# A decoder step on one core: product-key expert gates by indexed 4-byte adds in DRAM instead of one-hot products

## The chip, the core and the metric

The kernel runs on one core of a Trainium2 chip. The metric is device time in microseconds for one launch of the whole program. Five engines work beside each other and meet only at semaphores: TensorE (PE in the rows, with its weight loads as PEld), VectorE (DVE), ScalarE (ACT), GpSimd (POOL) and the queue SP, which only issues DMAs. POOL can issue DMAs too, and it alone issues the indexed ones.

## The reference, cut to what matters

One decoder layer over T = 592 tokens (16 meta tokens, 512 prompt tokens, 8 sequences of 8): mixers (gated linear attention and SSD), then the expert layer "PEER", then a norm. The change touches the expert layer, which works on the 576 tokens that aren't meta tokens:

```python
s1 = einsum('thd,kd->thk', q[:, :, 0], sub_k1); s2 = einsum('thd,kd->thk', q[:, :, 1], sub_k2)   # 8 heads, 128 keys each
v1, i1 = top_k(s1, 16);  v2, i2 = top_k(s2, 16)
cand = (v1[..., :, None] + v2[..., None, :]).reshape(n_tok, 8, 256)
sc, ci = top_k(cand, 16)
e = take_along_axis(i1, ci // 16) * 128 + take_along_axis(i2, ci % 16)    # one of 16384 experts, 128 slots a token
gate = softmax(sc)
hid = einsum('tkd,td->tk', u[e], t);  out = einsum('tk,tkd->td', gate * gelu(hid), v[e])
```

## The kernel before, in words

The kernel computes the expert layer densely for most tokens: it forms the hidden value of every token with all 16384 experts, multiplies by a gate matrix that is zero except at the chosen experts, and multiplies by all of v. TP = 576 tokens take part in the u products; TA = 448 of them go through the dense v products, and the last TBK = 128 are done by gathering the 128 chosen rows of v each ("slots").

**The u stage.** 128 blocks n, each with 128 experts. SP loads the block's u into one of four places of `ring` (`load_u`). ACT copies it rounded to fp32r (the high part, `split_u`, line 1030), another engine subtracts to get the low part (POOL, line 1573), and PE runs `split_product` (line 776): 8 x 3 x 2 = 48 products of 288 columns. `usp` has two places for the pair. ACT applies gelu into `gl` and SP stores it to `hidden_scratch` in DRAM.

**Routing.** Beside the first blocks, in five tiles of up to 128 tokens, PE computes `scores(i)` (16 small products), ACT copies them to `s12`, and DVE finds the top 16 of each half and head, the top 16 of 256 candidates, and by comparisons and sums (lines 1419 to 1423) the expert numbers e1, e2; then it divides the gates by their sum. ACT does the exponential (line 1072) in between. `scores(i)` stands ahead of quad 3i of the u blocks (a quad is four blocks). Tile 0 is the 128 tokens of the gathered path. The picks of tiles 1 to 4 are turned by PE (`turn_picks`) into e1T, e2T, gT.

**Gates by one-hot products.** From quad 17 on, two blocks of 16 tokens a quad, 28 in all: DVE makes a one-hot of e1 and one of e2 (lines 1450, 1451, each 128 x 2048), multiplies the first by two of three bf16 parts of the gate (line 1454), POOL by the third (line 1577), PE runs `gate_block` (line 835, 48 bf16 products), ACT copies the result to `stage` (line 1081), and SP stores it to `gates_scratch` (1 MB each), laid out (16 groups, 128, 448 tokens, 8).

**The v stage.** 128 blocks: SP loads v, the hidden block (`xn`) and, once for eight blocks, gates (`G`, 1.8 MB); DVE multiplies hidden by gate (`gate`, line 1472), ACT and DVE split v and the product in high and low parts, PE runs `second(n)` (line 866): 24 products of 448 columns. POOL issues the 128 + 128 gathers for the last 128 tokens (`pick_hid` line 1600, `pick_row` line 1593), and DVE adds the rows (line 1496). After the last block follow the add to h, a norm and the store.

**Ahead of all that**, SP loads the weights of 36 projections one by one into `ring` (`load_w`, line 394, 512 KB each, four places), each once PE is done with the projection four before it. Every instruction of an engine's list runs in the order written; the lists are unrolled or run in `Fori` loops.

## Time and profile before

| | us |
|---|---|
| median of 3 runs | 2213.4 |
| lowest, highest of 3 | 2199.16, 4156.74 |
| the profiled execution's own time | 2213.47 |
| span of the profiled execution | 2211.7 |

The profile is of one execution; its span starts and ends with the core's instructions, and 1.8 us of its own time lie around it. A row of a group of instructions gives its busy time, the mean of one in ns, and then the idle time of the engine just before them and what ended it. A row of a timeline gives start, duration (both us), what ran, and in brackets how long its engine had been idle and for whom. In the table by stretches, the bracketed x is the count of instructions, PEclk the clock that TensorE was granted as a share of full speed, and the last two the mean busy share of the 16 DMA engines and their rate.

### The profile page before, as it was taken

To read this page: it belongs to the slowest core of one execution; us is meant where nothing else is said; L and a number is where in the kernel's file an instruction comes from. 1 tells how busy PE (TensorE), PEld (TensorE's weight loads), DVE (VectorE), ACT (ScalarE), POOL (GpSimd) and SP (SyncE) were. 2 spreads that over 40 slices of the span, in tenths; PEclk is the share of its full clock that TensorE was granted. 3 is DMA by queue.
4 is the path that set the end of the run, shared out by engine and by line. 5 is a ranking of instruction groups with operands and counts; after the bars stand their busy time and mean duration, and the time that the engine had idled before them with its cause. 6 is when DMAs were issued, how large, how long until landed. Compare 5 with 4: busy or idle time off the path is not lost.

```text
span 2211.7 us, 34613 instructions
## 1 busy us (share of the span) xinstructions
PE 2108.4 (95%) x13720; PEld 1925.0 (87%) x13720; DVE 1576.2 (71%) x2188; ACT 659.0 (30%) x1062; POOL 1007.1 (46%) x452
## 2 busy tenths in 40 slices
PE   6999998798999999999999999999999999999996
PEld 3578777666999999999999998999899999999995
DVE  2335364635098898894899999992588888888884
ACT  2224112211223323323333332323333333333331
POOL 0023210201333333343887887973866665666300
PEclk8999997799999999999999999999999999999998
DMA  3011012022233333333455455546898989989861
GB/s 139 10 58 67 29 31 79 1 82 82 87 119 120 119 134 120 119 129 121 160 166 164 161 164 161 166 155 214 305 319 310 338 306 330 319 299 347 311 212 44
DMA packets 169054, 364.94 MB, mean 165 GB/s; under 512 B 18529, under 2 KB 92786, under 8 KB 166258
## 3 DMA queue, kind: packets, MB, share of 16 engines
q1 hardware_dynamic: 146418, 296.26, 38.9%
q0 software_dynamic: 22528, 67.19, 8.7%
q8 instruction: 74, 1.21, 0.2%
q14 instruction: 34, 0.28, 0.0%
HBM read 290.21 MB, written 73.18 MB: 164 GB/s over the span
## 4 chain that ended last, share of the span: by engine, by line
PE 55%; issue 24%; POOL 13%; DVE 5%; ACT 1%; DMA 1%; SPq 0%; POOLq 0%; DVEq 0%; ACTq 0%
PE bank L866 28%; POOL usp L1573 10%; PE bank L517 8%; PE bank L776 5%; PE bank L746 3%; POOL oneA L1577 3%; PE bank L551 2%; PE bank L503 1%; DVE oneA L1454 1%; PE bank L622 1%; PE bank L835 1%; DVE sq L1131 1%; PE bank L593 1%; DVE xn L1134 1%; PE bank L638 1%
## 5 line engine op out<-in xcount | busy, mean ns | idle before, releaser
L776 PE MATMUL bank<-xh,usp 128*128 128x288 f32 x4320 | 761.5, 297 | 7.0 <-POOL usp L1573 3.7
L776 PEld LDWEIGHTS bank<-xh,usp 128*128 128x128 f32 x4320 | 638.7, 189 | 9.5 <-POOL usp L1573 4.9
L866 PE MATMUL bank<-W,vsp 128*128 128x448 f32 x3072 | 635.0, 368 | 1.1 <-DVE W L1482 1.1
L866 PEld LDWEIGHTS bank<-W,vsp 128*128 128x128 f32 x3072 | 576.5, 188 | 59.3 <-issue 1.4
L1573 POOL TENSOR_TENSOR usp<-ring,usp 128x1024 fp32r<-128x1024 f32 x128 | 405.6, 3173 | 391.3 <-ACT usp L1030 391.3
L776 PE MATMUL bank<-xl,usp 128*128 128x288 f32 x2160 | 462.7, 296 | 0.0
L776 PEld LDWEIGHTS bank<-xl,usp 128*128 128x128 f32 x2160 | 348.6, 189 | 0.0
L1030 ACT ACTIVATE usp<-ring 128x1024 fp32r<-128x1024 f32 x128 | 135.6, 1060 | 611.9 <-PE bank L776 611.9
L1593 POOL DMA_INDIRECT picked<-in_v,row_index x128 | 173.9, 1359 | 181.4 <-DVE acc L1496 163.9
L1477 DVE TENSOR_TENSOR vsp<-ring,vsp 128x1024 fp32r<-128x1024 f32 x128 | 157.7, 1232 | 129.1 <-ACT vsp L1094 115.2
L1454 DVE TENSOR_TENSOR oneA<-hotA,gparts 128x2048 bf16<-128x2048 bf16 x56 | 226.7, 4087 | 0.0
L517 PE MATMUL bank<-xn,ring 128*128 128x296 f32 (+1 forms) x672 | 215.8, 445 | 10.8 <-DVE xn L1134 7.8
L1600 POOL DMA_INDIRECT hid_b<-hidden_scratch,hid_index x128 | 180.6, 1411 | 49.5 <-issue 38.7
L1094 ACT ACTIVATE vsp<-ring 128x1024 fp32r<-128x1024 f32 x128 | 135.5, 1058 | 130.6 <-PE bank L866 116.2
L1098 ACT ACTIVATE W<-sq 128x448 fp32r<-128x448 f32 x128 | 74.3, 581 | 296.9 <-DVE sq L1472 294.7
L1472 DVE TENSOR_TENSOR sq<-xn,G 128x448 f32<-128x448 f32 x128 | 140.5, 1098 | 31.0 <-DMA xn<-hidden_scratch 31.0
L1496 DVE SCALAR_TENSOR_TENSOR acc<-picked,w_b,acc 128x1024 f32<-128x1024 f32 x126 | 161.6, 1288 | 0.2
L1577 POOL TENSOR_TENSOR oneA<-hotA,gparts 128x2048 bf16<-128x2048 bf16 x28 | 152.1, 5433 | 0.0
L517 PEld LDWEIGHTS bank<-xn,ring 128*128 128x128 f32 x672 | 115.3, 194 | 39.7 <-issue 17.8
L1450 DVE TENSOR_TENSOR hotA<-cst,e1T 128x2048 bf16<-128x2048 f32 x28 | 111.3, 3976 | 15.2 <-PE bank L835 15.2
L1451 DVE TENSOR_TENSOR oneB<-cst,e2T 128x2048 bf16<-128x2048 f32 x28 | 114.7, 4096 | 0.0
L1533 POOL TENSOR_TENSOR E<-E,qT 128x2048 f32<-128x2048 f32 (+1 forms) x7 | 29.1, 4163 | 181.0 <-ACT qT L908 114.2
(237 smaller groups left out, 2001.8 us busy)
## 6 DMA issues: line engine op xcount, KB each, us to landing
ring<-in_u SPq DMA_DIRECT2D x128, 512.0 KB
ring<-in_v SPq DMA_DIRECT2D x128, 512.0 KB
hidden_scratch<-gl SPq DMA_DIRECT2D x128, 288.0 KB, 2.1
gates_scratch<-stage SPq DMA_DIRECT2D x28, 1024.0 KB, 5.6
G<-gates_scratch SPq DMA_DIRECT2D x16, 1792.0 KB
xn<-hidden_scratch SPq DMA_DIRECT2D x128, 224.0 KB
ring<-in_wproj SPq DMA_DIRECT2D x36, 512.0 KB
h<-in_xT SPq DMA_DIRECT2D x16, 296.0 KB, 4.5
```

The costliest lines, as they stand in the source:

```text
L517: mm = pe.matmul(bank[2 * (n % 2) + x][:, 0:half], ring[:, n % 4, k * P:(k + 1) * P], src[:, k, at + x * half:at + (x + 1) * half], start= ...
L776: mm = pe.matmul(bank[b + y][:, 0:PHALF], w, src[:, k, y * PHALF:(y + 1) * PHALF], start=(k == 0 and w is hi and src is xh), stop=(k == KT ...
L866: mm = pe.matmul(bank[(k + 4) % 8][:, 0:TA], w, W[:, n % 4, z, :], start=(n == 0 and w is hi and z == 0), stop=(n == NE - 1 and w is lo))
L1030: act.activation(usp[:, j % 2, 0, :], ring[:, j % 4, :], ACT.Copy).then_inc(uhi_ready, 1)
L1454: ins = dve.tensor_tensor(oneA[:, x, z, :, :], hotA[:, x, :, :], bc(gparts[:, z, bass.ds(b * TB, TB)], 2, NK), ALU.mult)
L1472: dve.tensor_tensor(sq[:, n % 2, 0:TA], xn[:, n % 8, 0:TA], G[n // GRP % 2][:, :, n % GRP], ALU.mult).then_inc(gated, 1)
L1477: dve.tensor_tensor(vsp[:, n % 4, 1, :], ring[:, n % 4, :], vsp[:, n % 4, 0, :].bitcast(F32), ALU.subtract).then_inc(vlo_ready, 1)
L1496: ins = dve.scalar_tensor_tensor(acc[:, x % 2, :], picked[:, x % NROW, :], w_b[:, x:x + 1], acc[:, x % 2, :], ALU.mult, ALU.add)
L1573: pool.tensor_tensor(usp[:, j % 2, 1, :], ring[:, j, :], usp[:, j % 2, 0, :].bitcast(F32), ALU.subtract).then_inc(ulo_ready, 1)
L1577: pool.tensor_tensor(oneA[:, j, 2, :, :], hotA[:, j, :, :], bc(gparts[:, 2, bass.ds((b + j) * TB, TB)], 2, NK), ALU.mult).then_inc(third_r ...
L1593: pool.indirect_dma_start(picked[:, x % NROW, :], None, rows_of_v, bass.IndirectOffsetOnAxis(ap=row_index[:, x:x + 1], axis=0)).then_inc(r ...
L1600: pool.indirect_dma_start(hid_b[:, x:x + 1], None, hid_flat, bass.IndirectOffsetOnAxis(ap=hid_index[:, x:x + 1], axis=0)).then_inc(picked_ ...
```

## The change

- The four temporaries of the one-hot way, `turn_picks`, `gate_block`, `gates_out`, `store_gates`, `one_hots` and POOL's third product go. `gates_scratch` becomes (128 blocks, 128, 448).
- A tile `zero` is set once by POOL. SP writes zeros over `gates_scratch` with 32 DMAs, four behind each of the weight loads 4 to 11, in pieces of 224 floats.
- Tiles are renumbered: the four of the dense path come first (128, 128, 128, 64 tokens), the gathered 128 tokens last. `scores(0)` stands ahead of the first quad, `scores(i + 1)` behind quad 4i; ACT copies tile i + 1's scores after quad 4i + 1 and the exponential of tile i.
- DVE keeps each tile's gates (`gate_val`) and their places (`gate_at`). POOL adds them with indexed DMAs of one column each, a 4-byte float for each token: 128 of them a tile (8 heads x 16), 512 in all. Between two heads of one tile it waits until the first head's 16 have landed; the later four heads of tile i - 1 and the first four of tile i are issued alternately.
- POOL makes the low parts of u for blocks 0 to 15; DVE makes the other 112, in the midst of the routing of tiles 1 to 4, one for each 6.0 us of work by the program's own count (`after`), the rest in a row after it. `usp` has four places instead of two, and ACT's high part is for block n + 4 instead of n + 2, and follows the gelu.
- `G` is loaded block by block (224 KB each) into eight places: the first eight by POOL once all adds have landed, the others by SP ahead of `load_hid`.

```diff
@@ SP
+            for n in range(4):
                 load_w(n)
+            sp.wait_ge(zero_ready, 1)
+            for n in range(4, 12):
+                load_w(n)
+                for g in (2 * n - 8, 2 * n - 7):
+                    for y in range(2):
+                        sp.dma_start(gates_dram[g * GRP:(g + 1) * GRP, :, y * (TA // 2):(y + 1) * (TA // 2)].rearrange("n p t -> p n t"),
+                                     zero[:, :, :].broadcast_to([P, GRP, TA // 2])).then_inc(zeroed, 16)
...
+            def load_gates(n):
+                sp.dma_start(G[:, n % 8, :], gates_dram[n, :, :]).then_inc(hid_loaded[n % 8], 16)
...
-            load_gates(1)
+            wait_gates_added(sp)
@@ PE
+            scores(0)
+            for i in range(TILES):
+                pooled = ROUTE_QUADS * i < POOL_SPLITS // 4
+                quad(ROUTE_QUADS * i, pooled, first=(i == 0))
+                if i + 1 < TILES:
+                    scores(i + 1)
                 with pe.Fori(ROUTE_QUADS * i + 1, ROUTE_QUADS * (i + 1)) as q:
-                    quad(q)
+                    quad(q, pooled)
+            with pe.Fori(ROUTE_QUADS * TILES, NE // 4) as q:
+                quad(q, False)
@@ ACT
-                    split_u(n + 2, j + 2, q)
                     gelu(n, j, None if first else q)
+                    split_u(n + 4, j, q + 1)
...
                 quad(ROUTE_QUADS * i, first=(i == 0))
+                quad(ROUTE_QUADS * i + 1)
                 act.wait_ge(sm_arg, i + 1)
                 act.activation(e12[0:r, 2, :, :], e12[0:r, 2, :, :], ACT.Exp).then_inc(sm_exp, 1)
+                if i + 1 < TILES:
+                    copy_scores(i + 1)
@@ DVE
+            def split_u(n):
+                dve.wait_ge(uhi_ready, n + 1)
+                dve.tensor_tensor(usp[:, n % NU, 1, :], ring[:, n % 4, :], usp[:, n % NU, 0, :].bitcast(F32), ALU.subtract
+                                  ).then_inc(ulo_ready, 1)
+            def after(us):
+                worked[0] += us
+                while worked[0] >= PITCH:
+                    split_u(next_split[0])
+                    next_split[0] += 1
+                    worked[0] += 1.3 - PITCH
...      # after(1.5) behind each of the 16 top16 of 128, after(3.3) behind each of the 8 of 256,
...      # after(3.3) and after(7.5) twice in the picks; tiles 1 to 4 only
+                    dve.tensor_tensor(gate_val[0:r, i, :, :], e12[0:r, 2, :, :], bc(den[0:r, 1, :], 2, TOPK), ALU.mult
+                                      ).then_inc(gates_ready, 1)
+                    link(dve.scalar_tensor_tensor(w_b[0:r, :], e2, float(NK), e1, ALU.mult, ALU.add))
+                    dve.tensor_scalar(gate_at[0:r, i, :], w_b[0:r, :], float(TA), col, ALU.mult, ALU.add
+                                      ).then_inc(gates_ready, 1)
+            for n in range(next_split[0], NE):
+                split_u(n)
...
-                dve.tensor_tensor(sq[:, n % 2, 0:TA], xn[:, n % 8, 0:TA], G[n // GRP % 2][:, :, n % GRP], ALU.mult
+                dve.tensor_tensor(sq[:, n % 2, 0:TA], xn[:, n % 8, 0:TA], G[:, n % 8, :], ALU.mult
@@ POOL
+            for n in range(POOL_SPLITS):
+                pool.wait_ge(uhi_ready, n + 1)
+                pool.tensor_tensor(usp[:, n % NU, 1, :], ring[:, n % 4, :], usp[:, n % NU, 0, :].bitcast(F32), ALU.subtract
+                                   ).then_inc(ulo_first, 1)
+            def add_gates(i, hh):
+                r = peer_rows(i)
+                if hh > 0:
+                    pool.wait_ge(gates_added[i], 16 * TOPK * hh)
+                for x in range(hh * TOPK, (hh + 1) * TOPK):
+                    pool.indirect_dma_start(gates_flat, bass.IndirectOffsetOnAxis(ap=gate_at[0:r, i, x:x + 1], axis=0),
+                                            gate_val[0:r, i, hh, x - hh * TOPK:x - hh * TOPK + 1], None, compute_op=ALU.add
+                                            ).then_inc(gates_added[i], 16)
+            pool.wait_ge(zeroed, 16 * 2 * NGRP)
+            for i in range(TILES):
+                if i < TILES - 1:
+                    pool.wait_ge(gates_ready, 2 * (i + 1))
+                for hh in range(PH // 2):
+                    if i >= 1:
+                        add_gates(i - 1, PH // 2 + hh)
+                    if i < TILES - 1:
+                        add_gates(i, hh)
+            wait_gates_added(pool)
+            for n in range(8):
+                pool.dma_start(G[:, n, :], gates_dram[n, :, :]).then_inc(g_first[n // 4], 16)
```

## Rows read from the trace of the kernel before

**Rows 1.** The page, part 1: busy time of each engine, share, instructions

```profile
PE 2108.4 (95%) x13720; PEld 1925.0 (87%) x13720; DVE 1576.2 (71%) x2188; ACT 659.0 (30%) x1062; POOL 1007.1 (46%) x452
```

**Rows 2.** Busy time by stretch: stretch, length, PE, PEld, DVE, ACT, POOL, PEclk, DMA, GB/s

```profile
600.80:1060.00 459.20, 457.44 (x3448) 455.82 (x3449) 386.01 (x1156) 142.69 (x254) 175.33 (x70) 1.00 0.36 123
1060.00:1510.00 450.00, 434.42 (x3967) 430.35 (x3966) 422.34 (x104) 146.15 (x276) 370.66 (x83) 0.98 0.51 164
...
1544.60:2180.50 635.90, 634.82 (x3074) 576.60 (x3073) 501.47 (x515) 205.60 (x253) 354.49 (x256) 1.00 0.83 296
2180.50:2211.70 31.20, 12.92 (x42) 8.37 (x40) 15.60 (x20) 7.66 (x11) 0.00 (x0) 0.75 0.20 79
```

**Rows 3.** ACT's timeline: high parts of u, each started by a finished block

```profile
617.29 1.06 ACT L1030 ACTIVATE usp<-ring 128x1024 fp32r<-128x1024 f32 x1 [3.31 <-PE bank L776]
...
674.98 1.07 ACT L1030 ACTIVATE usp<-ring 128x1024 fp32r<-128x1024 f32 x1 [4.82 <-PE bank L776]
...
681.29 1.06 ACT L1030 ACTIVATE usp<-ring 128x1024 fp32r<-128x1024 f32 x1 [4.66 <-PE bank L776]
...
691.29 1.06 ACT L1030 ACTIVATE usp<-ring 128x1024 fp32r<-128x1024 f32 x1 [4.51 <-PE bank L776]
```

**Rows 4.** Groups of instructions between 1060 and 1510 us

```profile
L1454 DVE TENSOR_TENSOR oneA<-hotA,gparts 128x2048 bf16<-128x2048 bf16 x52 | 213.3, 4141 | 0.0
...
L835 PE MATMUL bank<-oneB,oneA 128*128 128x128 bf16 x1344 | 86.1, 228 | 13.1 <-DVE oneA L1454 13.1
L835 PEld LDWEIGHTS bank<-oneB,oneA 128*128 128x128 bf16 x1344 | 81.2, 103 | 16.1 <-issue 14.5
```

**Rows 5.** DVE's timeline in the routing of tile 0, beside POOL's low parts

```profile
606.41 0.29 DVE L1390 MAX8 v<-s 128x8 f32<-128x128 f32 x1 [51.54 <-ACT s L1064]
...
631.53 2.38 DVE L1404 TENSOR_TENSOR cand<-v 128x256 f32<-128x256 f32 x1
...
636.20 0.41 DVE L1404 TENSOR_TENSOR cand<-v 128x256 f32<-128x256 f32 x1
...
659.42 0.29 DVE L1411 TENSOR_TENSOR e<-v 128x128 f32<-128x128 f32 x1
...
684.67 0.28 DVE L1425 TENSOR_REDUCE den<-e 128x8 f32<-128x128 f32 x1 [3.17 <-ACT e L1072]
```

**Rows 6.** The page, part 5: the low part of v on DVE

```profile
L1477 DVE TENSOR_TENSOR vsp<-ring,vsp 128x1024 fp32r<-128x1024 f32 x128 | 157.7, 1232 | 129.1 <-ACT vsp L1094 115.2
```

**Rows 7.** POOL's timeline: a low part of u beside routing

```profile
612.03 2.40 POOL L1573 TENSOR_TENSOR usp<-ring,usp 128x1024 fp32r<-128x1024 f32 x1 [5.57 <-ACT usp L1030]
```

**Rows 8.** POOL's timeline, indexed gathers of 128 x 4 bytes; last row, DVE's timeline

```profile
1550.66 0.95 POOL L1600 DMA_INDIRECT hid_b<-hidden_scratch,hid_index  x1 [0.30 <-issue]
...
1556.93 0.95 POOL L1600 DMA_INDIRECT hid_b<-hidden_scratch,hid_index  x1 [0.30 <-issue]
1558.19 1.67 POOL L1600 DMA_INDIRECT hid_b<-hidden_scratch,hid_index  x1 [0.30 <-issue]
...
1575.45 1.22 POOL L1593 DMA_INDIRECT picked<-in_v,row_index  x1 [0.30 <-issue]
...
1557.81 1.23 DVE L1477 TENSOR_TENSOR vsp<-ring,vsp 128x1024 fp32r<-128x1024 f32 x1 [7.92 <-issue]
```

**Rows 9.** Groups on POOL between 1600 and 2050 us

```profile
L1600 POOL DMA_INDIRECT hid_b<-hidden_scratch,hid_index x104 | 150.1, 1443 | 31.7 <-issue 31.7
L1593 POOL DMA_INDIRECT picked<-in_v,row_index x103 | 139.0, 1350 | 130.6 <-DVE acc L1496 116.4 <-issue 12.5 <-DVE acc L1493 1.7
```

**Rows 10.** The page, part 6, DMA issues: count, KB each, us from issue to landing

```profile
hidden_scratch<-gl SPq DMA_DIRECT2D x128, 288.0 KB, 2.1
gates_scratch<-stage SPq DMA_DIRECT2D x28, 1024.0 KB, 5.6
```

**Rows 11.** SP's timeline, weight loads 4 to 11, and ACT's copy of projection 11

```profile
105.86 65.26 SPq L394 DMA_DIRECT2D ring<-in_wproj  x8
...
222.06 0.72 ACT L908 ACTIVATE sz<-bank 128x296 f32<-128x296 f32 x2
```

More of the change, by code:

```diff
@@ L125, in constants @@
         "eps": np.full((P, 1), EPS),
-        "gcol": TA + r[:, None],
+        "column": np.stack([peer_cols(i).start + r for i in range(TILES)], axis=1),
     }
@@ L157, in build @@
         cst = sb(base, "cst", [P, CONST_N])
+        zero = sb(base, "zero", [P, 1, TA // 2])
         prm = sb(base, "prm", [P, PARAM_N])
@@ L289, in build @@
         hid_stored = [sem(f"hid_stored{s}") for s in range(4)]
-        g_loaded = [sem(f"g_loaded{s}") for s in range(2)]
+        g_first = [sem(f"g_first{s}") for s in range(2)]
         stored = sem("stored")
@@ L822, in quad @@
                     mm.then_inc(hid_done, 1)
-                    if b is not None and j < 2:
-                        gate_block(b + j, j, first=(isinstance(b, int) and b + j == 0))
-            def gate_block(b, x, first=False):
-                pe.wait_ge(one_hot_ready, b + 1)
-                pe.wait_ge(third_ready, b + 1)
-                for q in range(TB // 4):
-                    if not first:
-                        pe.wait_ge(gate_copied, b * (TB // 4) + q - 3)
-                    for t in range(4):
-                        for z in range(3):
-                            mm = pe.matmul(bank[4 + q][:, t * NK:(t + 1) * NK], oneA[:, x, z, 4 * q + t, :],
-                                           oneB[:, x, 4 * q + t, :], start=(z == 0), stop=(z == 2))
-                    mm.then_inc(gate_done, 1)
@@ L1044, in quad, with copy_scores @@
                     act.wait_ge(hid_done, n + 1)
-                    split_u(n + 2, j + 2, q)
                     gelu(n, j, None if first else q)
-                    if b is not None and j < 2:
-                        gates_out(b + j, j, first=isinstance(b, int))
-            def copy_picks(i):
-                act.wait_ge(e_turned, i)
-                for x, dst in enumerate((e1T, e2T, gT)):
-                    ins = act.activation(dst[:, peer_cols(i)], bank[4][:, x * P:x * P + peer_rows(i)], ACT.Copy)
-                ins.then_inc(e_copied, 1)
-            split_u(0, 0, 0)
-            split_u(1, 1, 0)
-            for i in range(TILES):
+                    split_u(n + 4, j, q + 1)
+            for j in range(4):
+                split_u(j, j, 0)
+            def copy_scores(i):
                 r = peer_rows(i)
@@ L1526, in _ @@
         def _(pool):
+            pool.memset(zero[:, :, :], 0.0).then_inc(zero_ready, 1)
             pool.wait_ge(proj_act, 2)
@@ L1567, in _ @@
                                    ).then_inc(qlo_ready, 1)
-            def quad(q, b=None):
-                for j in range(4):
-                    pool.wait_ge(uhi_ready, q * 4 + (j + 1))
-                    pool.tensor_tensor(usp[:, j % 2, 1, :], ring[:, j, :], usp[:, j % 2, 0, :].bitcast(F32), ALU.subtract
-                                       ).then_inc(ulo_ready, 1)
-                    if b is not None and j < 2:
-                        pool.wait_ge(one_hot_step, b + (j + 1))
-                        pool.tensor_tensor(oneA[:, j, 2, :, :], hotA[:, j, :, :],
-                                           bc(gparts[:, 2, bass.ds((b + j) * TB, TB)], 2, NK), ALU.mult
-                                           ).then_inc(third_ready, 1)
```

214 lines of the change are left out of this document (68 added, 146 removed).

## The prediction, made before the changed kernel ran

> **What bounds the kernel now.** I read the page's busy times first, then the table by stretches, then the waits and timelines of each stretch. TensorE is busy 95% of the span [rows 1], but the stages differ. In the u stage with routing (600.8 to 1060) and in the v stage (from 1544.6, 635.9 us) PE hardly pauses; the v stage is bound by PE's own products, DVE at 79% and the DMA engines at 83% beside it [rows 2]. The middle, 1060 to 1510, is where one-hot gates are made: DVE is busy 422 of 450 us, POOL 371, and PE is 16 us short of full [rows 2]. So PE sets the time nearly everywhere, and what can be gained is PE work that goes away plus those waits.
>
> The price of a block of u comes from ACT's timeline. A high part starts when a block is done, and nine blocks lie between 617.29 and 674.98: 57.7 / 9 = 6.41 us a block. The step from 681.29 to 691.29 has `scores` in it: 10.0 - 6.4 = 3.6 us [rows 3].
>
> **PE after the change.** The stage runs from 600.8 to 1544.6, 943.8 us [rows 2]. Without gate products and turns there remain 128 blocks x 6.41 = 820.5 and five `scores` x 3.6 = 18.0, together 838.5 us. That is 105.3 us less, if nothing new holds PE. Cross-check: 28 gate blocks with 86.1 us of busy product records (they overlap a little, so some 75 to 86) and the waits in front of them, 13.1 for DVE and up to 16.1 for loads of weights [rows 4]: 104 to 115. The v stage would then begin at 600.8 + 838.5 = 1439.3 instead of 1544.6.
>
> **DVE as maker of low parts.** One low part is 1024 columns, two inputs, fp32r out: the same shape as the low part of v, 1.23 us [rows 6]. Routing of tile 0 takes 606.4 to 659.4 up to the exponential's argument and ends at 681.5 in its picks (684.67 less the 3.17 of waiting) [rows 5]: 75.1 us, with POOL's low parts in its way (the same `cand` operation takes 2.38 or 0.41 us [rows 5]). The program counts 16 x 1.5 + 8 x 3.3 + 2 x (3.3 + 7.5) = 72.0 us for it, and takes a low part for each 4.7 of them (6.0 - 1.3): 15.3 a tile. In real time that is at most 4.7 x 75.1 / 72.0 + 1.3 = 6.2 us a low part, under PE's 6.41. So DVE keeps up, and mostly waits for ACT's high part, which comes three blocks ahead of need (19 us of cover). The 2 us of small operations at a tile's end fit in there. Cost 0; if the pitch were 7 us instead, 61 low parts would bring (7 - 6.41) x 61 - 19 = 17 us. ACT waits for a tile's exponential argument with the gelus of later blocks behind it. DVE reaches it with low part 26 (tile 1), and ACT stands at it after block 23; PE stalls only from block 26, for whose banks it needs gelu 24. A few us of slack at worst, cost 0. SP's load of u for block n + 4 waits for DVE instead of POOL, and still has more than one block of time, against 2 to 6 us that loads and stores take to land [rows 10]. One low part in the first sixteen costs POOL 2.40 us of each 6.41 [rows 7], nothing for PE.
>
> **Zeroing.** 32 stores, 29.4 MB, go in between loads 4 to 11 on one queue. Loads 4 to 11 start within 65.3 us from 105.9, and projection 11, the last behind zeros, must be fed some 11 us before ACT copies it at 222.1 [rows 11]. 29.4 + 4.2 MB in about 105 us is 320 GB/s. The v stage moves 296 GB/s at a share of 0.83, so 357 GB/s at full share [rows 2]; the 1 MB gate stores in 512-byte pieces take 5.6 us, 187 GB/s with the latency in it, 300 without 2.1 us of it [rows 10]. At 357 there is no stall; at 300, 33.6 / 0.3 = 112 us, 7 us late; at 187 it would be 75 us late, which would leave 2183. The pieces here are 896 bytes and many DMAs are in flight, which is nearer to the first: I take 0, and keep 75 as the far end.
>
> **POOL's adds** decide. An indexed add does not occur in the trace; the nearest is the indexed gather of 128 x 4 bytes. Alone, with DVE idle, five periods take 1556.93 - 1550.66: 1.25 us each (0.95 busy, 0.30 between). When DVE starts its two-input operations at 1557.8, nine take 17.26: 1.92 each [rows 8]. Over the v stage the mean is (1.443 + 1.350) / 2 + 0.31 = 1.70, with DVE busy 79% [rows 2, 9]. So DVE's two-input operations stretch them, by (1.70 - 1.25) / 0.79 = 0.57 us per unit of such share. In the u stage DVE has such work for about 37 of 98 us a tile (15.3 low parts x 1.23 = 19, candidates 8 x 0.41 = 3, and an estimated 15 of the 22 us of picks), then 1.23 of each 6.41: 1.25 + 0.57 x 0.38 = 1.46 us an add while routing lasts, 1.25 + 0.57 x 0.19 = 1.36 after. I take these. Bounds: 1.25 and 1.70.
>
> The Trainium skill says of this ("SBUF — State Buffer", section "SBUF: two separate sides") that GpSimd, which writes the descriptors, is fully blocked from a shared port while such a DVE operation runs. Here the trace agrees only in part: at a DVE share of three quarters the period grows 1.5 times, where full blocking would make it four times. By that rule the adds would take about 1.25 / 0.62 = 2.0 us during routing and 1.25 / 0.81 = 1.54 after it, and the time would be about 2260, the upper end of the first rival.
>
> Now the chain. Block 1 ended at 617.3 [rows 3]; POOL's last low part (15) follows block 11, at 617.3 + 10 x 6.41 + 3.6 = 685.0, plus some 4 us for gelu, high part (1.06) and low part (2.40): 689. Gates of tile 0 are ready at 684, the picks' end and 2 us of small operations. Four heads of tile 0: 64 x 1.46 = 93, and three waits for landing; a store's 2.1 us [rows 10] each: 788. Tile 1's gates are ready at 684 + 15.3 x 6.41 + 3.6 = 786, tile 2's at 888, so from here POOL is never starved. 128 more: 187, to 975. The next 128: 79 until routing ends at 1091, 49 x 1.36 = 67 after, to 1158. The next 128: 174, to 1332. The last 64 x 1.36 = 87 and four landings, 8: 1427. First loads of G: four issues and a landing, 4 x 1.25 + 2.1 = 7, then `gate` and the split of W, 3 us: W is ready at 1437. PE is free at 1439.3. The adds just fit. In general W is ready at 715.5 + 512 a, a being the mean period of an add (here 1.41); each 0.1 us of a is 51 us. Tile 3 has 64 tokens, which may make 128 of the adds cheaper; no row shows it, bounds 0 to 60 us earlier.
>
> **The v stage** keeps its 24 products a block. `G` now moves in 1792-byte pieces like `xn`, same bytes, 0 us; DVE's `gate` can only get cheaper. The tail from 2180.5 [rows 2] stays.
>
> **Sum.** 2211.7 - 105.3 = 2106.4 of span; the profiled execution took 1.8 us more than its span, so 2108.2, and I say 2108. That execution (2213.47) is the median of the runs shown (2213.4), whose lowest is 14 us under it.
>
> **Rivals.**
> - *Adds late but bearable*: a from 1.44 to 1.70, as in the v stage. Time 2108 + 512 x (a - 1.41): at 1.70, 715.5 + 870.4 = 1585.9, which is 41 us later than the v stage began before, 2255. For it: all gathers beside a busy DVE cost this. Against it: DVE has half that load here. It costs more than it brings from a = 1.62 on.
> - *An add is dearer than a gather* (ends slower). An add must fetch what lies in DRAM beside what it brings, so POOL has more to write for it. If it writes twice as much: 2 x 0.95 + 0.30 = 2.20 alone, about 2.36 with DVE: 715.5 + 1208 = 1924, 379 us later than before, 2593. It decides from a = 1.71 (2% slower). The mirror of it is a landing that outlasts 16 adds of the other tile (23 us); then the waits between heads pace it. For it: nothing in the trace shows an add. Against: the DMA engines are idle two thirds of this time [rows 2]. The Trainium skill ("Collectives: The Full Stack", section "The bandwidth ceiling: the fold count and why AG ≠ RS ≠ AR") says that an add emits two read descriptors per piece where a copy emits one, and that this halved the rate; no row here shows it, and by it the time would be this rival's.
> - *PE isn't freed*: low parts on DVE at 7 us or the zero stores late, 10 to 30 us given back: 2118 to 2138. Speaks against it: 6.2 us by the sum above.
>
> **Chances.** Forecast (adds hidden or nearly, 2095 to 2125) 0.48; given back in part, 2125 to 2169, 0.12; within 2% of before, 2169 to 2258, 0.15 (the upper part of the first rival); slower, 0.25. Two per cent, 44 us, is about what a measurement of this kernel can tell from no change. Faster 0.60, same 0.15, slower 0.25. The likeliest case's own range is 2090 to 2125. The range for 8 in 10 runs from 2090, by the spread of the runs and cheaper half tiles, to 2260, the gather's worst price; dearer adds stay outside.
>
> **What would show it.** Right: PE's blocks of 6.41 us throughout, v products starting near 1440, POOL's adds at 1.3 to 1.5 us in a row until about 1425, no stall of PE around 110 to 220. Wrong: PE idle ahead of the v stage for the G loads, with POOL still adding, and a period over 1.5 us; idle gaps in the add stream at head ends (landing); PE waiting for low parts from DVE; PE waiting for `ring` near 150 to 220.

## The result, and the profile after

| | us |
|---|---|
| changed kernel, median of 4 runs (lowest, highest) | 2424.61 (2419.52, 2429.45) |
| kernel before, median of 4 runs on the same chip | 2207.03 |
| ratio, with its 95% interval | 1.100 [1.096, 1.105] |
| forecast | 2108 |

One of the four executions of the kernel before took 4156.74 us; it stands apart from the other three (2199.16 to 2213.4) and is left out of the ratio. The change makes the kernel 10% slower; the time lies 317 us above the forecast. The page of the changed kernel (busy times, then groups with busy us, mean ns, idle time before and its releaser, then a DMA row with KB and us to landing):

```profile
PE 2027.9 (84%) x12364; PEld 1845.5 (76%) x12364; DVE 1158.1 (48%) x2191; ACT 607.7 (25%) x943; POOL 1335.7 (55%) x833
...
L1521 POOL DMA_INDIRECT gates_scratch<-gate_val,gate_at x512 | 851.3, 1663 | 184.5 <-issue 155.9
L823 PE MATMUL bank<-W,vsp 128*128 128x448 f32 x3072 | 643.4, 370 | 315.3 <-DVE W L1420 299.2
...
L1410 DVE TENSOR_TENSOR sq<-xn,G 128x448 f32<-128x448 f32 x128 | 79.2, 619 | 317.7 <-DMA G<-gates_scratch 317.7
...
gates_scratch<-zero SPq DMA_DIRECT2D x32, 896.0 KB, 10.5
```

PE's busy share falls from 95% [rows 1] to 84%, although its busy time fell by 80 us. It waits once for 299.2 us, for W; W's maker waits for `G`, and `G` for the last of 512 adds. The adds hold POOL for 851 us, 1.66 us each. The table by stretches (columns as in [rows 2]) sets the same in time:

```profile
0.00:600.80 600.80, 535.71 (x2952) 421.15 (x2953) 242.84 (x387) 146.20 (x252) 97.36 (x41) 0.92 0.32 108
600.80:1439.00 838.20, 836.61 (x6302) 835.03 (x6301) 451.28 (x1263) 246.76 (x426) 658.99 (x370) 1.00 0.58 128
1439.00:1736.60 297.60, 0.00 (x0) 0.00 (x0) 4.06 (x6) 1.18 (x3) 236.18 (x167) 0.50 0.19 6
1736.60:2395.80 659.20, 643.04 (x3071) 581.12 (x3072) 444.29 (x516) 205.91 (x253) 343.15 (x256) 0.98 0.84 285
```

The u stage is full and ends at 1437 (last product 1436.98). Then of all engines only POOL has work for 298 us. The v stage takes 659.2 us instead of 635.9 [rows 2]. So there are two losses: 297.4 us by which the v stage begins later than 1439.3, and 23.3 us inside it. With a tail 0.4 us shorter, 2108.2 + 297.4 + 23.3 - 0.4 = 2428.5, and that execution took 2426.6 of span and 1.8 around it, 2428.4. The two losses are the whole difference between forecast and time.

**The first loss.** POOL's timeline of the changed kernel (start, us, and the idle time before), beside DVE's low parts and, in the last two rows, with no DVE work:

```profile
1271.28 1.55 POOL L1521 DMA_INDIRECT gates_scratch<-gate_val,gate_at  x1 [0.31 <-issue]
1273.14 2.31 POOL L1521 DMA_INDIRECT gates_scratch<-gate_val,gate_at  x1 [0.30 <-issue]
1275.75 1.55 POOL L1521 DMA_INDIRECT gates_scratch<-gate_val,gate_at  x1 [0.30 <-issue]
1277.60 1.55 POOL L1521 DMA_INDIRECT gates_scratch<-gate_val,gate_at  x1 [0.30 <-issue]
1279.45 2.39 POOL L1521 DMA_INDIRECT gates_scratch<-gate_val,gate_at  x1 [0.30 <-issue]
...
1499.10 1.55 POOL L1521 DMA_INDIRECT gates_scratch<-gate_val,gate_at  x1 [0.30 <-issue]
1500.96 1.55 POOL L1521 DMA_INDIRECT gates_scratch<-gate_val,gate_at  x1 [0.30 <-issue]
```

and DVE's timeline of the same stretch:

```profile
1272.80 1.23 DVE L1338 TENSOR_TENSOR usp<-ring,usp 128x1024 fp32r<-128x1024 f32 x1 [5.09 <-ACT usp L987]
1279.19 1.23 DVE L1338 TENSOR_TENSOR usp<-ring,usp 128x1024 fp32r<-128x1024 f32 x1 [5.17 <-ACT usp L987]
```

An add of 128 tokens holds POOL for 1.55 us where the gather of the same size held it for 0.95 [rows 8]; the pause of 0.30 is the same. That is a period of 1.85, and 1.73 for the tile of 64 tokens (1.43 busy). A low part that is running when an add starts lengthens the add, by 0.76 and 0.84 us in these rows and by 1.02 at most after routing; the mean distance between 1100 and 1400 us is 2.12. The rows also show by what rule. The low part of 1279.19 ends at 1280.42 and the add beside it at 1281.84, 1.42 us later; the one of 1272.80 ends at 1274.03 and its add at 1275.45, again 1.42 later. After 1095 us an add starts beside a running low part 47 times, and 46 times it ends 1.41 to 1.44 us behind the low part's end. So the add stands still until the low part is over and has only 0.13 of its 1.55 us behind it by then. An add that has started first is not lengthened, and neither is the low part (POOL's timeline, then DVE's):

```profile
1118.96 1.55 POOL L1521 DMA_INDIRECT gates_scratch<-gate_val,gate_at  x1 [0.30 <-issue]
```

```profile
1119.20 1.23 DVE L1338 TENSOR_TENSOR usp<-ring,usp 128x1024 fp32r<-128x1024 f32 x1 [3.81 <-ACT usp L987]
```

**The second loss.** PE's timeline at the start of the v stage of the changed kernel:

```profile
1736.65 25.25 PE L823 MATMUL bank<-W,vsp 128*128 128x448 f32 x111 [299.24 <-DVE W L1420]
...
1772.10 0.53 PE L823 MATMUL bank<-W,vsp 128*128 128x448 f32 x1 [0.68 <-issue]
1774.20 0.53 PE L823 MATMUL bank<-W,vsp 128*128 128x448 f32 x1 [1.57 <-issue]
...
1784.00 0.53 PE L823 MATMUL bank<-W,vsp 128*128 128x448 f32 x1 [0.85 <-issue]
1786.10 74.18 PE L823 MATMUL bank<-W,vsp 128*128 128x448 f32 x351 [1.57 <-issue]
```

From 1762 to 1786 PE starts 17 products, mostly one each 1.4 to 2.8 us, where it did 111 in the 25 us before, and the profile shows nothing that it waits for ("issue"). POOL's timeline of the same kernel shows what runs meanwhile:

```profile
1760.60 0.95 POOL L1551 DMA_INDIRECT hid_b<-hidden_scratch,hid_index  x1 [0.30 <-issue]
1761.85 0.94 POOL L1544 DMA_INDIRECT picked<-in_v,row_index  x1 [0.31 <-issue]
1763.10 0.95 POOL L1551 DMA_INDIRECT hid_b<-hidden_scratch,hid_index  x1 [0.30 <-issue]
...
1780.60 0.95 POOL L1551 DMA_INDIRECT hid_b<-hidden_scratch,hid_index  x1 [0.31 <-issue]
1815.52 0.95 POOL L1544 DMA_INDIRECT picked<-in_v,row_index  x1 [33.98 <-DVE acc L1431]
```

Indexed gathers go 1.25 us apart, without a break, until 1781; PE recovers at 1786. The experiments take up both losses.

### The profile page after: what moved, and what is told of

It is laid out like the page before. It is cut to its first block, busy times and chain, and to the rows that moved or that the text cites. A ratio compares the mean times of both kernels' runs of the same rounds, so it can differ in the third digit from the quotient of the medians.

```text
span 2426.6 us, 31564 instructions
## 1 busy us (share of the span) xinstructions
PE 2027.9 (84%) x12364; PEld 1845.5 (76%) x12364; DVE 1158.1 (48%) x2191; ACT 607.7 (25%) x943; POOL 1335.7 (55%) x833
## 3 DMA queue, kind: packets, MB, share of 16 engines
q0 software_dynamic: 88576, 69.29, 17.7%
## 4 chain that ended last, share of the span: by engine, by line
PE 51%; POOL 35%; issue 8%; DVE 3%; DMA 2%; ACT 1%; SPq 0%; DVEq 0%; POOLq 0%; ACTq 0%
POOL gates_scratch L1521 34%; PE bank L823 27%; PE bank L510 8%; PE bank L769 5%; PE bank L739 3%; DMA gates_scratch<-gate_val,gate_at 2%; PE bank L544 2%; PE bank L496 1%; PE bank L615 1%; DVE sq L1071 1%; PE bank L586 1%; DVE xn L1074 1%; PE bank L631 1%; PE bank L726 1%; PE bank L696 0%
## 5 line engine op out<-in xcount | busy, mean ns | idle before, releaser
L1521 POOL DMA_INDIRECT gates_scratch<-gate_val,gate_at x512 | 851.3, 1663 | 184.5 <-issue 155.9
L823 PE MATMUL bank<-W,vsp 128*128 128x448 f32 x3072 | 643.4, 370 | 315.3 <-DVE W L1420 299.2
L769 PE MATMUL bank<-xh,usp 128*128 128x288 f32 x4320 | 752.0, 296 | 1.4 <-DVE xl L1326 1.4
L1338 DVE TENSOR_TENSOR usp<-ring,usp 128x1024 fp32r<-128x1024 f32 x112 | 136.8, 1221 | 341.9 <-ACT usp L987 318.2
L1544 POOL DMA_INDIRECT picked<-in_v,row_index x128 | 149.8, 1171 | 216.4 <-DVE acc L1434 165.5
L1410 DVE TENSOR_TENSOR sq<-xn,G 128x448 f32<-128x448 f32 x128 | 79.2, 619 | 317.7 <-DMA G<-gates_scratch 317.7
L994 ACT ACTIVATE gl<-bank 128x288 f32<-128x288 f32 x256 | 91.3, 409 | 542.9 <-PE bank L769 484.8
L1551 POOL DMA_INDIRECT hid_b<-hidden_scratch,hid_index x128 | 193.3, 1510 | 48.0 <-issue 38.7
L1420 DVE TENSOR_TENSOR W<-sq,W 128x448 fp32r<-128x448 f32 x128 | 79.0, 617 | 0.1
L1502 POOL TENSOR_TENSOR xl<-xn,xh 128x576 fp32r<-128x576 f32 x4 | 7.7, 1951 | 119.9 <-ACT xh L973 119.9
```

Of the source, the lines that this page charges most:

```text
L769: mm = pe.matmul(bank[b + y][:, 0:PHALF], w, src[:, k, y * PHALF:(y + 1) * PHALF], start=(k == 0 and w is hi and src is xh), stop=(k == KT ...
L823: mm = pe.matmul(bank[(k + 4) % 8][:, 0:TA], w, W[:, n % 4, z, :], start=(n == 0 and w is hi and z == 0), stop=(n == NE - 1 and w is lo))
L994: ins = act.activation(gl[:, j, y * PHALF:(y + 1) * PHALF], bank[2 * (j % 2) + y][:, 0:PHALF], ACT.Gelu_apprx_tanh)
L1338: dve.tensor_tensor(usp[:, n % NU, 1, :], ring[:, n % 4, :], usp[:, n % NU, 0, :].bitcast(F32), ALU.subtract).then_inc(ulo_ready, 1)
L1521: pool.indirect_dma_start(gates_flat, bass.IndirectOffsetOnAxis(ap=gate_at[0:r, i, x:x + 1], axis=0), gate_val[0:r, i, hh, x - hh * TOPK:x ...
L1544: pool.indirect_dma_start(picked[:, x % NROW, :], None, rows_of_v, bass.IndirectOffsetOnAxis(ap=row_index[:, x:x + 1], axis=0)).then_inc(r ...
```

## The experiments

All kernels are the changed kernel with one edit; e12 joins the edits of e3 and e9. The kernel before took 2195.1 us beside the first eight, 2201.2 beside e9 to e11.

**e1: plain indexed writes in place of adds (gates that meet on one place aren't summed); e2: gathers of the same places (no gate is written at all).**

```diff
 pool.indirect_dma_start(gates_flat, IndirectOffsetOnAxis(ap=gate_at[0:r, i, x:x + 1], axis=0),
-                        gate_val[...], None, compute_op=ALU.add)
+                        gate_val[...], None)                                          # e1
-pool.indirect_dma_start(gates_flat, IndirectOffsetOnAxis(...), gate_val[...], None, compute_op=ALU.add)
+pool.indirect_dma_start(gate_in[0:r, i, x:x + 1], None, gates_flat, IndirectOffsetOnAxis(...))  # e2
```

> The changed kernel with its 512 indexed DMAs as plain writes instead of adds; it leaves out the sum where two heads of a token chose the same expert. In the changed kernel one add, alone on POOL, takes 1.55 us and 0.30 between (period 1.85), and 2.12 beside DVE's low parts, and PE waits 299 us. Theory A: the price lies in the adding (two things to fetch for each write). Then a plain write costs what a gather does: 0.95 us alone, period 1.25, some 1.45 beside DVE, the adds end near 1440 and the time is 2120 to 2160. Theory B: the price lies in the direction, an index on the DRAM side of a write. Then 1.55 stays, and the time stays at 2410 to 2430.

> The changed kernel with each of the 512 adds replaced by a gather of the same 128 places into SBUF, so the gates stay zero. Both theories on adding and direction: 0.95 us alone, period 1.25, 1.36 to 1.46 beside DVE as the prediction took, end near 1427, time 2105 to 2140. Rival: the u stage itself (its DMA traffic, DVE's low parts) makes indexed DMAs dear; then the gather too would take 1.5 us or more and the time would stay above 2250.

Measured: 2774.0 and 2744.1 us. The trace by line of e1 and of e2 (minimum, median, maximum in ns, first and last start):

```profile
L1521 POOL DMA_INDIRECT gates_scratch<-gate_val,gate_at x512: 891/958/1913, 688.9 to 1626.0; - x171
```

```profile
L1522 POOL DMA_INDIRECT gate_in<-gates_scratch,gate_at x512: 894/947/1931, 683.3 to 1627.8; - x171
```

Two things follow. A plain write costs what a gather does, 0.96 and 0.95 us, so the direction is free and **the accumulation is the price**: 1.55 against 0.96. The pages (part 3, packets of POOL's own queue, MB, share) show that an add is cut up finer, in the changed kernel and then in e1:

```profile
q0 software_dynamic: 88576, 69.29, 17.7%
```

```profile
q0 software_dynamic: 39424, 69.29, 7.6%
```

That is 96 packets more for each of the 512 transfers. Whether their making is what holds POOL 0.6 us longer, no run tests.

The second thing: the kernel became slower, not faster, and the last write started at 1626, although 512 x 1.26 is only 645 us. The stretch from 857 to 1020, in e1 and then in the changed kernel, both in the columns of [rows 2]:

```profile
857.00:1020.00 163.00, 37.13 (x137) 28.18 (x135) 17.10 (x83) 4.60 (x7) 122.85 (x127) 0.53 0.05 11
```

```profile
857.00:1020.00 163.00, 163.00 (x1230) 162.71 (x1229) 128.57 (x404) 54.07 (x91) 137.96 (x79) 1.00 0.59 126
```

While plain writes run 1.26 us apart, PE does 137 products instead of 1230, DVE 83 operations instead of 404, and the DMA engines move a tenth. "Starve" below stands for this. POOL starves with them: it waits 282 us in three places for `gate_at`, which the hindered routing delivers late. PE's timeline of e1 in that stretch looks like the v stage's stall above:

```profile
896.46 0.40 PE L769 MATMUL bank<-xl,usp 128*128 128x288 f32 x1 [2.40 <-issue]
899.26 0.40 PE L769 MATMUL bank<-xh,usp 128*128 128x288 f32 x1 [2.40 <-issue]
902.06 0.40 PE L769 MATMUL bank<-xh,usp 128*128 128x288 f32 x1 [2.40 <-issue]
```

That was not expected by any theory, and e5 to e7 and e9 to e11 are about it.

**e3, e4: four and six of the eight heads are added** (the gates of the others are left out).

```diff
-                eng.wait_ge(gates_added[i], 16 * PH * TOPK)
+                eng.wait_ge(gates_added[i], 16 * 4 * TOPK)
-                for hh in range(PH // 2):
+                for hh in range(4 // 2):              # 6 in e4, here and in the other lines
-                        add_gates(i - 1, PH // 2 + hh)
+                        add_gates(i - 1, 4 // 2 + hh)
```

> The changed kernel with the adds of heads 0 to 3 only (256 of 512); the gates of heads 4 to 7 are left out. Theory: POOL's stream of adds alone holds the v stage back, so 256 x 2.1 us from 689 on end near 1250, all hidden; PE goes from the u stage into the v stage at 1439 and the time is 2108 (2100 to 2125), the sum of the prediction without the adds. Rival: something else of the change (four places of usp, G loaded by block, the start of the v stage) costs too; then 2125 or more, with PE's idle time or a longer v stage showing it.

> The changed kernel with the adds of six heads (384 of 512); the gates of heads 6 and 7 are left out. Theory: the time follows the number of adds once they outlast PE's 1439 us, at the mean of 2.0 us. 128 adds fewer end 128 x 1.8 to 2.1 = 230 to 270 us earlier, near 1480, v stage from about 1490, time 2155 to 2200. Rival: the landings between heads pace the stream; then the time falls by less than 200 us, since as many heads' ends remain in the stretches that are not alternated.

Measured: 2122.5 and 2178.8 us. With 256 adds the last starts at 1241, and PE goes from u (1437.8) to v without a gap. With 384 it starts at 1476.1 and PE waits 57.2 us. From 384 to 512 adds the span grows by 2426.6 - 2177.0 = 249.6 us, 1.95 us an add: once POOL ends last, the number of adds times their period sets the time (the v stage took 1.8 us of the 249.6). In both, the v stage took 652.6 and 657.4 us: the second loss is there without the first.

**e8: a one-input operation on DVE beside the adds** (the true low part of u is left out).

```diff
-dve.tensor_tensor(usp[:, n % NU, 1, :], ring[:, n % 4, :], usp[:, n % NU, 0, :].bitcast(F32), ALU.subtract)
+dve.tensor_scalar(usp[:, n % NU, 1, :], ring[:, n % 4, :], 2.0 ** -14, None, ALU.mult)
```

> The changed kernel, with DVE's low part of u made by an operation of one input (ring x 2^-14) in place of the two-input subtraction; the true low part of u is left out. Theory A (two-input operations of DVE are what stretch an add from 1.85 to about 2.12 us): after routing, where the low parts are DVE's only work, the period goes to 1.85 to 1.90; over the stage 40 to 100 us fall away, and the time is 2320 to 2385. Rival (any operation of DVE on wide rows stretches them, or the adds stretch for another reason, the u loads or the stores of hidden rows): the period stays at 2.05 to 2.15 and the time at 2410 to 2430.

Measured: 2366.7 us; the last add starts at 1674.7 instead of 1723.0. POOL's and then DVE's timeline of e8:

```profile
1256.76 1.55 POOL L1520 DMA_INDIRECT gates_scratch<-gate_val,gate_at  x1 [0.30 <-issue]
1258.61 1.90 POOL L1520 DMA_INDIRECT gates_scratch<-gate_val,gate_at  x1 [0.30 <-issue]
```

```profile
1259.73 0.69 DVE L1338 TENSOR_SCALAR usp<-ring 128x1024 fp32r<-128x1024 f32 x1 [5.71 <-issue]
```

The mean distance between 1100 and 1400 us is 1.89, not 2.12, so DVE's low parts do stretch the adds, and theory A's numbers came in. But two inputs are not the condition: the one-input operation stretches them too, by 0.35 us here for its 0.69 us. An add that starts beside it ends 1.43 us behind its end, as with the subtraction; the shorter the operation, the fewer adds it meets and the sooner it lets them go. One difference stays open: after 1095 us the subtraction never lengthened an add that had started first, and this operation does when it starts 1.0 to 1.2 us into the add, as in these rows, but not at 0.2 to 0.4. (13 of the 62 us by which this execution is shorter than the profiled one of the changed kernel belong to the v stage, as much as PE's pace makes, see the last section.)

**e7: the picks held back.**

```diff
+            pool.wait_ge(block_done, 6)
             for x in range(TOPK):
                 pick_hid(x)
```

> The changed kernel, with POOL's picks of hidden values (16 indexed gathers in a row, 1.25 us apart) held back until block 6 of the v stage is done. Theory A (the gathers in a row starve PE at the start of the v stage, where VectorE and the weight loads are just behind): held back, they run where eight blocks of G, xn and v lie ready or DVE stretches them, the v stage goes from 659 us back to about 636 to 642, time 2400 to 2408 in place of 2425. Rival: the v stage is longer because the first blocks' loads or G come late; then it stays near 659 and the time near 2425; or the stall only moves with the gathers to block 6, again 2425.

Measured: 2431.0 us, v stage 663 us. The stall moved with the gathers, as the second half of the rival has it. PE's timeline of e7:

```profile
1736.95 52.33 PE L823 MATMUL bank<-W,vsp 128*128 128x448 f32 x239 [298.28 <-DVE W L1420]
1789.94 1.09 PE L823 MATMUL bank<-W,vsp 128*128 128x448 f32 x4 [0.66 <-issue]
...
1815.98 44.27 PE L823 MATMUL bank<-W,vsp 128*128 128x448 f32 x201 [0.17 <-issue]
```

The gathers start at 1770.6 instead of 1740.2, the stall at 1789 instead of 1762: some 20 us behind them in both. The first blocks' loads, which were the rival's first half, are not the cause: PE does 239 products without a pause before this stall.

**e9: the picks paced.** Behind each indexed gather, two memsets of POOL, each waiting for the one before.

```diff
+            def pause():
+                for _ in range(2):
+                    if paced_n[0]:
+                        pool.wait_ge(paced, paced_n[0])
+                    paced_n[0] += 1
+                    pool.memset(zero[:, 0, 0:224], 0.0).then_inc(paced, 1)
```

> The changed kernel with its 512 adds, and two memsets of 224 columns on POOL after each indexed gather of the v stage (hidden values and rows of v). Theory A (indexed transfers 1.25 us apart hold up the issue of the other engines, while those some 1.8 us apart don't): the stall of PE near 1762 to 1786 disappears wherever the gathers fall, the v stage goes from 659 to 636 to 642 us, and the time from 2425 to 2400 to 2408. Rival (the gathers as such cost that, in whatever distance, or something else of the v stage): 655 to 665 us and about 2425, as when they were held back.

Measured: 2405.9 us. PE's timeline of e9:

```profile
1736.74 637.57 PE L823 MATMUL bank<-W,vsp 128*128 128x448 f32 x3072 [298.81 <-DVE W L1420]
```

All 3072 products of the v stage run without a pause, in 637.6 us instead of 659.2. POOL has more to do than before (1508.6 us busy instead of 1335.7), and the kernel is 19 us faster: the gathers 1.25 us apart were the cause of the second loss. (Both executions have the same pace of PE, see the last section.)

**e5, e10, e6: plain writes at growing distance; e11: smaller ones.** As e1 (duplicates of a place aren't summed), with memsets behind each write, of 8 columns (e5), 224 (e10) and twice 224 (e6). e11 is e1 with 16 of the 128 tokens in each transfer (the other tokens' gates are left out).

```diff
+                    for _ in range(2):                  # once in e5 and e10
+                        if paced_n[0]:
+                            pool.wait_ge(paced, paced_n[0])
+                        paced_n[0] += 1
+                        pool.memset(zero[:, 0, 0:224], 0.0).then_inc(paced, 1)      # 0:8 in e5
-                r = peer_rows(i)
+                r = 16                                  # e11 alone, without memsets
```

> The plain indexed writes of e1, and after each of them a small memset of 8 columns on POOL that waits for the memset before it (the gates aren't accumulated, so those that fall on one place twice are left out). Its purpose is the distance between two indexed transfers: 1.26 us in e1, about 1.4 to 1.5 here. Theory A (what starves PE, ACT, DVE and SP is that the next indexed transfer is issued with no more than 0.3 us of pause, whatever it moves): the starving shrinks or disappears, the stretch of plain writes shows a PE share well over the 23% of e1, and the time falls from 2774 to below 2400. Theory B (the cost lies in each plain transfer as such, 128 pieces of 4 bytes without a read of what is there): the same 512 transfers cost PE what they cost in e1, about 580 us, whatever lies between: about 2700 to 2774.

> Plain indexed writes as in e1 and e6, with one memset of 224 columns after each (gates that fall on one place twice aren't summed). It puts the distance near 1.55 us, between 1.45, where the other engines starved, and 1.82, where they did not. If the starving ends below 1.55: writes done by about 1500, PE full from 700 to 1000 and 1100 to 1400, the v stage from 1500 to 1520, time 2160 to 2230. If it ends above: PE at half in these stretches, time 2550 to 2720. A gradual effect would lie between, with PE at 60 to 90%.

> As the run before, but two memsets of 224 columns in a row after each plain indexed write (duplicates of a place left out again), for a distance of some 1.8 us or more, that of the adds of the changed kernel when VectorE is idle (1.85). Theory A (distance between transfers decides): no starving at all; POOL is done about when the adds are done in the changed kernel, if the distance is 1.85 to 2.1, and the time is 2330 to 2450, with PE busy in the u stage as there. Theory B (cost per plain transfer): still about 580 us of lost PE time, 2700 or more.

> Plain indexed writes without a pause as in e1, but each moves 16 of the 128 tokens (the gates of the other tokens are left out). Theory P (the other engines are held up by the 128 small pieces of each transfer, 100 pieces a us): with an eighth of the pieces PE keeps its blocks of 6.4 us and the time is 2105 to 2130. Theory I (each indexed transfer that POOL issues holds them up, however small it is): the same starving, PE at half between 700 and 1000, time 2600 or more. The add's own price: 16 rows at 0.90 us or less (64 rows took 0.90, 128 rows 0.96) say that nearly all of it is fixed.

Measured (the distance is from start to start, without the waits of over 4 us; PE is its busy share of 700 to 1000 and 1100 to 1400, and the column beside it its products there as a share of the 4520 of the changed kernel; at a lower clock a product takes longer, so the busy share hides part of the loss):

| | distance, us: median, mean | POOL busy with one | PE busy | PE's products | time, us |
|---|---|---|---|---|---|
| e11, 16 tokens | 1.15, 1.22 | 0.85 | 47% | 40% | 2773.8 |
| e1 | 1.26, 1.28 | 0.96 | 49% | 39% | 2774.0 |
| e5 | 1.27, 1.40 | 0.96 | 53% | 36% | 2707.4 |
| e10 | 1.43, 1.52 | 0.97 | 89% | 74% | 2331.3 |
| e6 | 1.77, 1.87 | 0.97 | 100% | 100% | 2325.3 |
| changed kernel, adds | 1.85, 1.99 | 1.55 | 100% | 100% | 2424.6 |

The shares come from these rows, of e11, e5, e10 and e6 in turn (columns as in [rows 2]):

```profile
700.00:1000.00 300.00, 126.68 (x787) 117.28 (x787) 84.70 (x272) 32.64 (x56) 144.20 (x169) 0.66 0.14 44
1100.00:1400.00 300.00, 155.20 (x1025) 146.76 (x1024) 104.65 (x300) 45.54 (x78) 114.26 (x130) 0.72 0.17 56
```

```profile
700.00:1000.00 300.00, 163.18 (x821) 137.58 (x819) 85.28 (x274) 32.74 (x56) 186.18 (x337) 0.65 0.15 44
1100.00:1400.00 300.00, 153.54 (x810) 131.44 (x809) 82.09 (x262) 30.95 (x53) 174.47 (x323) 0.66 0.14 43
```

```profile
700.00:1000.00 300.00, 274.05 (x1755) 255.31 (x1754) 184.93 (x597) 70.87 (x121) 257.54 (x379) 0.90 0.31 98
1100.00:1400.00 300.00, 259.72 (x1578) 239.34 (x1577) 85.88 (x176) 60.54 (x104) 262.16 (x396) 0.87 0.29 91
```

```profile
700.00:1000.00 300.00, 300.00 (x2268) 299.07 (x2267) 234.22 (x724) 92.20 (x159) 260.56 (x451) 1.00 0.39 125
1100.00:1400.00 300.00, 300.00 (x2252) 300.00 (x2251) 58.05 (x47) 79.17 (x142) 261.25 (x486) 1.00 0.40 129
```

So the distance decides. e5 hardly tested it: most of its transfers are 1.27 us apart, as in e1, its products are no more, and its time lies where theory B put it. It shows that a memset as such cures nothing. e10 came out at 1.43 and not at the 1.55 that I aimed at, and there a quarter of the products is missing; e6 at 1.77 loses none. No run lies between 1.43 and 1.77.

It isn't the number of tokens in a transfer: an eighth of them (e11) starves PE as much. It isn't the number of packets either. e11's page counts 39424 for POOL's queue, the same as e1's, so e11 alone could not rule them out; but the adds have 96 more each and starve nothing. (From the 384 adds of e4 to the 512 of the changed kernel the count grows by 88576 - 72192 = 16384, 128 for each add, which leaves 32 for a plain write: the adds pass 128 in 1.99 us, the writes of e1 32 in 1.28.) Nor is it the pause behind a transfer, as theory A of e5 has it: adds leave the same 0.30 us as e1's writes. The adds of the changed kernel are slow enough to be harmless.

**e12: what is left without both losses.** e3's 256 adds (half of the gates are left out) and e9's paced picks.

> 256 of the 512 adds as in e3 (the gates of the heads that aren't added are left out) and the paced gathers of e9. It shows what the rest of the change brings once both costs found so far are gone. Theory (the price of the adds and the stall of PE among the gathers are all that stood between the forecast and the time): the v stage takes 637 us as in e9, from 1437.8, and the time is 2102 to 2112, beside a forecast of 2108; 0.95 to 0.96 of the kernel before. Rival (the v stage of the changed layout costs more when it begins in the full clock, or the gates' store collides with it): near the 2122 of e3.

Measured: 2093.8 us, median of 4 executions, beside 2208.4 of the kernel before (7 executions), ratio 0.950 [0.947, 0.954]. PE's timeline of e12:

```profile
1436.63 622.75 PE L823 MATMUL bank<-W,vsp 128*128 128x448 f32 x3072
```

PE has no pause between u and v and none in v. The row is of the execution of 2090.85 us. The time is 8 us below the range that I gave, because v took 622.8 us and not 637; that is PE's pace in this execution (last section). So the rest of the change brings what the forecast said, once the adds fit under the u stage and the gathers are kept apart. It is no cure, since half of the gates are missing.

## Why the prediction was wrong, step by step

- **PE after the change: right.** The v stage could have begun at 1439.3; the last u product ended at 1437.0, 2 us earlier. e3 and e12 went from u to v at 1437.8 and 1436.6. Blocks stay at 6.41 us: the low parts above start 1279.19 - 1272.80 = 6.39 us apart.
- **DVE as maker of low parts: right.** PE is busy for 836.6 of 838.2 us; no rival of that kind occurred.
- **Zeroing: right.** From 0 to 600.8 PE is busy for 535.7 us, in the kernel before for 535.5; the DMA engines' share grew from 0.17 to 0.32 there. The far end of 75 us is off the table.
- **When the adds start: right.** 689 was said, 688.8 measured, and POOL never waited for gates of a later tile.
- **The price of an add: the step that failed.** The nearest row was the gather, 0.95 + 0.30 [rows 8], and I took it as the add's own base. Measured by the adds' mix, the base is (384 x 1.85 + 128 x 1.73) / 512 = 1.82 instead of 1.25. The size of the term for DVE's share was nearly right, though not its reasoning (see the shared port below): 1.41 - 1.25 = 0.16 forecast; the mean period is (1723.0 - 688.8) / 511 = 2.02, and 2.02 - 1.82 = 0.20, with 28.5 us of landing waits in it, 0.06 of the 0.20. The base alone is 0.57 x 512 = 292 us of the 297.
- **The bounds failed with it.** 1.25 to 1.70 were both prices of gathers. An operation that no row shows had bounds from one direction only, although the second rival stated the reason why an add can be dearer and said from where it decides (a = 1.71). That rival was right in its mechanism and too high in its price: POOL is busy 1.63 times as long (1.55 / 0.95), not twice, so 2.02 came in place of 2.36 and 2425 in place of 2593. The formula W = 715.5 + 512 a gives 1750 for 2.02; the 14 us over 1736.5 are landing waits that it counts a second time.
- **The Trainium skill on adds.** "Collectives: The Full Stack", section "The bandwidth ceiling: the fold count and why AG ≠ RS ≠ AR", has an add emit two reads where a copy emits one and the rate halved. Here the period grows 1.47 times (1.85 / 1.26), so the rule agrees in direction and is too strong for this case; the section speaks of large transfers between cores, and this case is about POOL's time for small ones. It spoke against the change, and it deserved more weight than one in four.
- **The Trainium skill on the shared port.** By "SBUF — State Buffer", section "SBUF: two separate sides", whichever of the two operations starts first has the shared ports for its whole length, and the other is fully blocked. For an add that finds a low part running the trace agrees: it ends 1.42 us after the low part, so it stood still for all but 0.13 us. The other way round the trace doesn't agree: the low part of 1119.20 took its usual 1.23 us inside an add. The prediction's test of the rule (four times the period at a DVE share of three quarters) counted every microsecond of DVE as blocked time, but in the changed kernel's stretch after routing only operations that were running when a transfer started cost anything.
- **The v stage: wrong by 23 us, of which the gathers explain 22** (659.2 to 637.6 in e9). The prediction put this term at nothing, since products and bytes stay and DVE's `gate` "can only get cheaper". It did get cheaper: 619 ns (L1410 above) against these of the kernel before, beside which stands PE's group there:

```profile
L1472 DVE TENSOR_TENSOR sq<-xn,G 128x448 f32<-128x448 f32 x128 | 140.5, 1098 | 31.0 <-DMA xn<-hidden_scratch 31.0
L866 PE MATMUL bank<-W,vsp 128*128 128x448 f32 x3072 | 635.0, 368 | 1.1 <-DVE W L1482 1.1
```

  But DVE's work also kept the gathers apart. The first 32 of them were on average 1.62 us apart in the kernel before, where PE paused once, for 1.1 us, in the whole stage, and 1.30 in the changed one. That the shorter `gate` is what brought them together is an inference; no run puts the old one back.
- **The gap in the old rows was no sign of it.** DVE was idle for 7.92 us, put down to "issue", before its low part of v at 1557.81 [rows 8]. It fits the starving at first sight, but ACT's timeline of the kernel before puts it down to the load of v:

```profile
1556.72 1.06 ACT L1094 ACTIVATE vsp<-ring 128x1024 fp32r<-128x1024 f32 x1 [6.75 <-DMA ring<-in_v]
```

  The low part waited for this high part, PE went on meanwhile (busy for 24.91 of the 26 us from 1549 to 1575), and the gap began at 1549.9, only 0.9 us after the first gather; in no run does the starving begin before 10 us.

## What to carry to other kernels

Price an indexed accumulate by itself, never by the gather beside it, and multiply first: with several hundred of them on one queue, half a microsecond each is the whole gain. When several engines are idle for "issue" at once, look at what another engine does without a pause at that moment; when it is one engine alone, follow its inputs a step back first. Back-to-back indexed transfers from POOL can take about as much time from PE as they take on POOL (e1: 512 x 1.26 = 645 us, and the v stage begins 645 us late, at 2083.9), and a little filler work between them can make a kernel faster; a faster transfer (e1) can make it slower by 350 us.

The runs also bound a better version: 384 adds would still be late (e4), 256 are hidden with 195 us to spare (last start 1241). Gates of 256 tokens by adds and of the other 192 by one-hot products would, by [rows 4], give PE back about 12 x (86.1 / 28) = 37 us; 2108 + 37 is about 2145, an estimate for PE's part alone, with the gathers of the v stage paced as in e9. It was not built.

## What the runs showed that I had not expected

- **Indexed transfers 1.15 to 1.3 us apart starve every other engine.** In e1, from 857 to 1020, PE does 11% of its products, DVE 21% of its operations, and the DMA engines' share is 0.05 in place of 0.59; the idle time stands as "issue". At 1.43 us (e10) the loss is a quarter of PE's products, at 1.77 (e6) nothing. It begins some time after the first transfer of a series, 10 to 22 us in the u stage (13 in e1, 688.9 to 702.2), 19 to 37 in the v stage (22 in the changed kernel, 1740.2 to 1762, and 19 in e7, 1770.6 to 1789), and ends within 6 us of the last (1780.6 and 1786.1), as if a stock were used up first. The cause is open; it is neither the size nor the direction of the transfers. PE's granted clock goes down after the pauses have begun: in e1 it is 1.00 from 690 to 700, 0.83 from 700 to 720, while PE is busy for two thirds of the time, and 0.50, its lower level of 1.2 GHz, from 730 to 780.
- **An indexed transfer is nearly all fixed cost.** 16, 64 and 128 tokens of a plain write hold POOL for 0.85, 0.90 and 0.96 us; an add of 64 and 128 tokens for 1.43 and 1.55. The tile of 64 tokens pays 94% of a full one.
- **PE has two paces in the v stage at full clock.** 485 or 495 products in 100 us, from one execution to the next and whatever the kernel: 486 in the profiled execution of before, 485 or 486 in the changed kernel, e1, e3, e4, e7, e9 and e10, 495 in e2, e5, e6, e8, e11 and e12. Over 3072 products that is 13 us, as much as lies between the fastest and the slowest of the seven runs of the kernel before beside e12 (2200.1 to 2213.6). That the seven differ for this reason is not shown, since only their times are kept. Differences below 13 us between single executions mean little here.
